# Attention's softmax blocks weighed, turned and copied four or two at a time, with smaller gate matmuls and a later conversion of query weights

## What is computed

```python
# rg_lru, 512 channels in 8 blocks of 64
r = sigmoid(block_diag_linear(x, w_a, b_a))
i = sigmoid(block_diag_linear(x, w_i, b_i))
# sparse attention: 16 heads of 64, blocks of 128 queries
proj = x @ w_in
gate = sigmoid(proj[..., 1024:])           # 16 heads x 3 branches = 48 columns
o = gate_c * o_c + gate_s * o_s + gate_w * o_w
# o_s and o_w: softmax(q k^T / 8 + relative bias, causal) v
# o_c: the same over 31 compressed keys
```

## Time and profile before

| | value |
|---|---|
| median of 3 runs | 2038.97 us (2037.82 to 2039.61) |
| the profiled execution's own time | 2038.9 us |
| its span | 2037.1 us |
| TensorE busy | 2018.7 us, 99% of the span |
| DVE busy | 1079.5 us, 53% |
| ACT busy | 829.4 us, 41% |
| GpSimd busy | 16.8 us, 1% |
| TensorE clock granted over the span | 0.996 of 2.4 GHz |

### The profile page before, as it was taken

How to read it: one execution, slowest core, us unless ns; L and a number is a source line. 1 busy time by engine, 2 the same in 40 slices (tenths; PEclk the granted TensorE clock), 3 DMA queues, 4 the chain that set the end, 5 groups by cost and what they waited for, 6 DMA issues and landing times.

```text
span 2037.1 us, 26626 instructions
## 1 busy us (share of the span) xinstructions
PE 2018.7 (99%) x10576; PEld 1697.4 (83%) x10576; DVE 1079.5 (53%) x1866; ACT 829.4 (41%) x1385; POOL 16.8 (1%) x31
## 2 busy tenths in 40 slices
PE   9999999999999999999999999999999999999998
PEld 7788888888888888889888888888788898888887
DVE  6665444443465465444744432387778666444323
ACT  5644333332334334334433322354777664333222
POOL 0000000000000000000000000000000000000000
PEclk9999999999999999999999999999999999999999
DMA  4223233323332222223233333353110023333232
GB/s 164 76 77 107 88 99 93 102 87 96 115 94 79 78 93 88 72 94 104 83 96 100 93 96 96 97 170 117 29 56 23 12 94 99 97 93 103 87 100 73
DMA packets 53546, 184.47 MB, mean 91 GB/s; under 512 B 6010, under 2 KB 8330, under 8 KB 53168
## 3 DMA queue, kind: packets, MB, share of 16 engines
q1 hardware_dynamic: 50976, 171.99, 27.4%
q0 software_dynamic: 2160, 10.63, 1.6%
q10 hardware_dynamic: 288, 0.17, 0.0%
HBM read 180.62 MB, written 2.14 MB: 90 GB/s over the span
## 4 chain that ended last, share of the span: by engine, by line
PE 93%; DVE 3%; issue 1%; ACT 1%; DVEq 0%; ACTq 0%
PE bank L518 70%; PE bank L538 6%; PE bank L687 6%; PE bank L1070 2%; PE bank L1052 1%; PE bank L927 1%; PE bank L1037 1%; PE bank L1038 1%; PE bank L915 1%; PE bank L963 1%; PE bank L1022 0%; DVE WL L1724 0%; DVE SS L2464 0%; PE bank L1023 0%; PE bank L1073 0%
## 5 line engine op out<-in xcount | busy, mean ns | idle before, releaser
L1724 DVE TENSOR_TENSOR WL<-RAW,WH 128x1024 fp32r<-128x1024 f32 (+1 forms) x320 | 384.0, 1204 | 459.1 <-ACT WH L1133 458.1
L518 PE MATMUL bank<-AH,WH 128*128 128x512 f32 x1456 | 568.5, 394 | 1.0 <-DVE XP L1779 1.0
L518 PE MATMUL bank<-AL,WH 128*128 128x512 f32 x1456 | 562.3, 390 | 0.0
L518 PE MATMUL bank<-AH,WL 128*128 128x512 f32 x1456 | 561.7, 390 | 0.0
L1133 ACT ACTIVATE WH<-RAW 128x1024 fp32r<-128x1024 f32 (+1 forms) x320 | 331.3, 1041 | 492.6 <-PE bank L518 418.4
L518 PEld LDWEIGHTS bank<-AH,WH 128*128 128x128 f32 x1456 | 273.3, 188 | 59.7 <-issue 4.0
L518 PEld LDWEIGHTS bank<-AH,WL 128*128 128x128 f32 x1456 | 273.4, 188 | 57.4
L518 PEld LDWEIGHTS bank<-AL,WH 128*128 128x128 f32 x1456 | 273.4, 188 | 55.2 <-issue 0.7
L1779 DVE TENSOR_TENSOR T<-bank,RS 128x512 f32<-128x512 f32 x156 | 106.3, 687 | 165.9 <-PE bank L518 165.9
L518 PE MATMUL bank<-HH,WH 128*128 128x512 f32 x484 | 188.3, 389 | 0.0
L518 PE MATMUL bank<-HLO,WH 128*128 128x512 f32 x484 | 188.3, 389 | 0.0
(11 more groups left out here) (400 smaller groups left out, 2835.2 us busy)
## 6 DMA issues: line engine op xcount, KB each, us to landing
RAW<-in_ffn_in SPq DMA_DIRECT2D x132, 512.0 KB, 3.6
RAW<-in_ffn_out SPq DMA_DIRECT2D x48, 512.0 KB, 3.5
RAW<-in_ret_t SPq DMA_DIRECT2D x32, 512.0 KB, 3.6
RAW<-in_ffn_out SPq DMA_DIRECT2D x24, 384.0 KB, 3.2
RAW<-in_ret_v SPq DMA_DIRECT2D x16, 512.0 KB, 3.7
RAW<-in_ret_out SPq DMA_DIRECT2D x16, 512.0 KB, 3.6
RAW<-in_w_in_t SPq DMA_DIRECT2D x13, 512.0 KB, 4.1
RAW<-in_nsa_t SPq DMA_DIRECT2D x9, 512.0 KB, 3.6
```

Of the source, the lines that this page charges most:

```text
L518: t = e.matmul(BANK[b][:, :], wt[:, sl], xx[:, slot(kk) if name == "nsa_out" else kk, :], start=kk == 0 and n == 0, stop=kk == kt - 1 and ...
L1724: e.tensor_tensor(WL[w][:, 0:n], RAW[r][:, 0:n], WH[w][:, 0:n], ALU.subtract).then_inc(w_low.did(v))
```

## The change

- **Joined blocks.** `JOINED = (4, 2, 1, 1)` by i. `lead(s)` is the first step of a joined group and `place(s)` puts the scores of a group side by side in one buffer of 512 columns. For i = 0 the four steps of a unit, for i = 1 its steps in pairs are multiplied by one DVE instruction (a tensor-by-tensor product with the weights broadcast), turned in one go of four transposes into one bank, and copied by one ACT instruction of 512 columns. For i = 2 and 3 nothing changes. DVE waits for the turn of step s - 9 only where both s and s - 9 lead a group.
- **Later query weights.** DVE's `before("nsa_t", ...)` stands two steps later (s = 4 and s % 16 = 11), the one for nsa_out at s = 107. ACT's stay.
- **Quadrant gates.** bd keeps only the 64 x 64 blocks. Each of the two matmuls of `lru_gates` becomes two of 64 rows by 64 columns. The halves of the second are swapped (rows 0 to 63 give partitions 64 to 127 and the other way round), so that the four use the four quadrants of the array. The wait for the second bank stands ahead of all four. ACT takes the second sigmoid in two instructions of 64 partitions. GpSimd clears nothing.
- **One gate tile.** For tile 8 of nsa_t DVE writes the low part of the 48 columns into columns 64 to 111 of the high part's blocks. Two passes of 8 matmuls replace three. DVE adds partitions 64 to 111 to 0 to 47 with a copy and an addition, and then scales.

The core of the diff:

```diff
@@ -367,6 +368,16 @@
         LAST = N + VALUES
+        JOINED = (4, 2, 1, 1)
+
+        def lead(s):
+
+            return s - s % JOINED[STEPS[s][1]]
+
+        def place(s):
+
+            keys = 128 * (STEPS[s][1] + 1)
+            return SS[lead(s) % NSS][:, (s - lead(s)) * keys:(s - lead(s) + 1) * keys]
...
@@ -439,13 +450,11 @@
         def pool_program(e):
-            e.memset(bd[:, :, :], 0.0).then_inc(zeroed.did("bd"))
-            e.wait_ge(*zeroed.at("bd"))
             e.wait_ge(s_x[7], 16)
...
                     rows = slice(64 * half, 64 * half + 64)
-                    e.dma_start(bd[rows, 4 * i:4 * i + 4, rows],
+                    e.dma_start(bd[rows, 4 * i:4 * i + 4, :],
                                 D[name].rearrange("(f a) i j -> a i f j", a=2)[half]).then_inc(s_bd, 16)
...
@@ -750,10 +759,12 @@
                 e.wait_ge(*lru_v.at(("conv", f)))
-                e.matmul(BANK[b][:, :], bd[:, f, :], y[:, :], start=True, stop=True).then_inc(
+                enter(b + 1, ("lru_i", f))
+                e.matmul(BANK[b][LOW, :], bd[LOW, f, :], y[LOW, :], start=True, stop=True)
+                e.matmul(BANK[b][UP, :], bd[UP, f, :], y[UP, :], start=True, stop=True).then_inc(
                     matmul.did(("lru_a", f)))
-                enter(b + 1, ("lru_i", f))
-                e.matmul(BANK[b + 1][:, :], bd[:, 4 + f, :], y[:, :], start=True, stop=True).then_inc(
+                e.matmul(BANK[b + 1][UP, :], bd[LOW, 4 + f, :], y[LOW, :], start=True, stop=True)
+                e.matmul(BANK[b + 1][LOW, :], bd[UP, 4 + f, :], y[UP, :], start=True, stop=True).then_inc(
                     matmul.did(("lru_i", f)))
...
@@ -981,9 +992,22 @@
+            def gate_tile():
+                u, b = p.first["nsa_t", 8], p.bank["nsa_t", 8]
+                w = p.slot[u]
+                enter(b, ("nsa_t", 8))
+                e.wait_ge(*w_low.at(u))
+                for kk in range(8):
+                    sl = slice(kk * 128, (kk + 1) * 128)
+                    e.wait_ge(*x_high.at(("q", kk)))
+                    e.matmul(BANK[b][:, :], WH[w][:, sl], AH[:, kk, :], start=kk == 0, stop=False)
+                    e.wait_ge(*x_low.at(("q", kk)))
+                    t = e.matmul(BANK[b][:, :], WH[w][:, sl], AL[:, kk, :], start=False, stop=kk == 7)
+                t.then_inc(matmul.did(("unit", u), ("nsa_t", 8)))
+
             for ht in range(2):
                 hidden(0, ht, range(16))
-            tile("nsa_t", 8, A, split_of("q"))
+            gate_tile()
             compressed(0)
...
@@ -1048,7 +1072,7 @@
                 e.wait_ge(*weighed.at(s))
-                for j in range(STEPS[s][1] + 1):
+                for j in range(JOINED[STEPS[s][1]] * (STEPS[s][1] + 1)):
                     t = e.transpose(b[:, ROWS[j]], SS[s % NSS][:, ROWS[j]], ident[:, :])
...
@@ -1061,20 +1085,22 @@
                     e.wait_ge(*free_a.at(("cmp", 1)))
-                e.wait_ge(*free_a.at(("turn", 4 * u + 3)))
+                e.wait_ge(*free_a.at(("turn", lead(4 * u + 3))))
                 out = [BANK[4 + f % 2][64 * hh:64 * hh + 64, ROWS[i]] for hh in range(2)]
...
                         for hh in range(2):
-                            e.matmul(out[hh], VS[:, j, c:c + 64], PT[(4 * u + 2 * br + hh) % NPT][:, ROWS[j]],
+                            v = 4 * u + 2 * br + hh
+                            e.matmul(out[hh], VS[:, j, c:c + 64],
+                                     PT[lead(v) % NPT][:, ROWS[(v - lead(v)) * (i + 1) + j]],
                                      start=br == 0 and j == 0, stop=False)
...
             for s in range(LAST):
-                if TURN <= s < N + TURN:
+                if TURN <= s < N + TURN and lead(s - TURN) == s - TURN:
                     turn(s - TURN)
...
@@ -1241,8 +1267,9 @@
                 e.wait_ge(*matmul.at(("lru_i", f)))
-                e.activation(g[:, :], BANK[b + 1][:, :], ACT.Sigmoid, bias=V("lru_bi", f)).then_inc(
-                    free_a.did(("lru_i", f)))
+                for own, other in ((LOW, UP), (UP, LOW)):
+                    e.activation(g[own, :], BANK[b + 1][other, :], ACT.Sigmoid,
+                                 bias=V("lru_bi_swapped", f)[other]).then_inc(free_a.did(("lru_i", f)))
...
@@ -1648,9 +1675,9 @@
                     compressed_values(s - 8)
-                if TURN <= s < N + TURN:
+                if TURN <= s < N + TURN and lead(s - TURN) == s - TURN:
                     v = s - TURN
-                    n = 128 * (STEPS[v][1] + 1)
+                    n = 128 * (STEPS[v][1] + 1) * JOINED[STEPS[v][1]]
                     e.wait_ge(*matmul.at(("turn", v)))
...
@@ -1721,6 +1748,11 @@
                     e.wait_ge(*w_high.at(v))
+                    if v == p.first["nsa_t", 8]:
+                        wide, raw = (t.rearrange("p (k c) -> p k c", c=128) for t in (WH[w][:, :], RAW[r][:, :]))
+                        e.tensor_tensor(wide[:, :, 64:112], raw[:, :, 0:48], wide[:, :, 0:48], ALU.subtract).then_inc(
+                            w_low.did(v))
+                        continue
                     e.tensor_tensor(WL[w][:, 0:n], RAW[r][:, 0:n], WH[w][:, 0:n], ALU.subtract).then_inc(w_low.did(v))
...
@@ -2368,8 +2400,12 @@
             e.wait_ge(*kv_a.at(("k", 7)))
-            e.tensor_tensor(T[1][0:48, :], BANK[p.bank["nsa_t", 8]][0:48, :], RS[0:48, :], ALU.mult).then_inc(
-                free_v.did(("nsa_t", 8)))
+            e.tensor_copy(T[1][0:48, :], BANK[p.bank["nsa_t", 8]][64:112, :]).then_inc(kv_v.did("low gates"))
+            e.wait_ge(*kv_v.at("low gates"))
+            e.tensor_tensor(T[1][0:48, :], T[1][0:48, :], BANK[p.bank["nsa_t", 8]][0:48, :], ALU.add).then_inc(
+                kv_v.did("gates"))
+            e.wait_ge(*kv_v.at("gates"))
+            e.tensor_tensor(T[1][0:48, :], T[1][0:48, :], RS[0:48, :], ALU.mult).then_inc(free_v.did(("nsa_t", 8)))
             e.wait_ge(*kv_a.at("kc"))
...
@@ -2459,9 +2495,9 @@
                 e.wait_ge(*matmul.at(("att", s)))
-                if s >= NSS:
+                if s >= NSS and lead(s) == s and lead(s - NSS) == s - NSS:
                     e.wait_ge(*matmul.at(("turn", s - NSS)))
-                e.tensor_tensor_reduce(SS[s % NSS][:, 0:keys], BANK[score_bank["att", s]][:, 0:keys], bias, -1.0,
+                e.tensor_tensor_reduce(place(s), BANK[score_bank["att", s]][:, 0:keys], bias, -1.0,
                                        -GUARD, ALU.add, ALU.min, NM[:, s % 8:s % 8 + 1]).then_inc(
...
@@ -2481,10 +2517,20 @@
                 _, i, hh, br = STEPS[s]
-                u, n = s // 4, 2 * hh + br
-                weighted = SS[s % NSS][:, 0:128 * (i + 1)]
+                u, n, keys = s // 4, 2 * hh + br, 128 * (i + 1)
+                weight = CF[:, u % 4, n:n + 1]
                 e.wait_ge(*weighed.at(("weights", u)))
-                e.tensor_scalar(weighted, weighted, CF[:, u % 4, n:n + 1], None, ALU.mult).then_inc(weighed.did(s))
+                if i > 1:
+                    weighted = SS[s % NSS][:, 0:keys]
+                    e.tensor_scalar(weighted, weighted, weight, None, ALU.mult).then_inc(weighed.did(s))
+                elif i == 1:
+                    weighted = SS[s % NSS][:, 0:512].rearrange("p (h k) -> p h k", h=2)
+                    by = bass.AP(weight.tensor, weight.offset, [weight.ap[0], [2, 2], [0, 256]])
+                    e.tensor_tensor(weighted, weighted, by, ALU.mult).then_inc(weighed.did(s))
+                else:
+                    weighted = SS[s % NSS][:, 0:512].rearrange("p (b h k) -> p b h k", b=2, h=2)
+                    by = bass.AP(weight.tensor, weight.offset, [weight.ap[0], [1, 2], [2, 2], [0, 128]])
+                    e.tensor_tensor(weighted, weighted, by, ALU.mult).then_inc(weighed.did(s))
...
@@ -2496,7 +2542,8 @@
                         weights_of((s - SCALE) // 4)
-                    weigh(s - SCALE)
+                    if lead(s - SCALE) == s - SCALE:
+                        weigh(s - SCALE)
                 for f in range(8):
...
@@ -2513,9 +2560,9 @@
                         query_low(query_after(s - 2 - half), half)
-                if queries_before(s):
-                    before("nsa_t", queries_before(s))
-                if s == 6 * PAIR + 9:
+                if s > 1 and queries_before(s - 2):
+                    before("nsa_t", queries_before(s - 2))
+                if s == 6 * PAIR + 11:
                     before("nsa_out", 0)
...
```

11 lines of the change are left out of this document (6 added, 5 removed).

## The result

The changed kernel takes 2042.44 us (median of 20 runs, 2037.87 to 2043.70), the kernel before 2038.18 us in the same comparison (20 runs, 2035.90 to 2040.69). The ratio is 1.0020, with a 95% interval of 1.0014 to 1.0026: the change makes the kernel 4 us slower. Forecast were 2033.2 us and a range up to 2038.0.

A forecast was written before the change was run, and what follows sets the result against it. TensorE, busy 2018.7 of 2037.1 us, was taken as the bound; 2038.9 - 2.3 (quadrant gates) - 1.8 (gate tile) - 1.6 (joined blocks and later query weights) = 2033.2 us, range 2028.0 to 2038.0.

The forecast's parts named there:

- rival A: Gate matmuls: the two row halves of a pair, writing one bank, do not overlap; 2036.5 us in all, chance 0.17.
- Part 1: Quadrant gates: a pair of gate matmuls takes 0.86 us instead of 1.72; -2.3 us, bounds -3.4 and +1.0.
- the first two places: Gate pairs after tiles 8 and 9: 0.5 us saved each, of which at most 0.89 us together arrives.
- The third place: Two gate pairs after the token-wise product: 1.72 - 0.35 = 1.4 us saved, arriving in full.
- Part 2: One gate tile: 8 of 24 matmuls go, 8 x 0.228 = -1.8 us; bounds -1.8 and 0.
- parts 3 and 4: Attention, joined blocks and later query weights: +0.9 - 0.6 - 1.5 - 0.4, about -1.6 us; bounds -8 and +8.
- 0.11 us each, alone or joined; I count nothing: Transposes in attention: their number stays 320 and each costs 0.11 us, alone or joined, so no change.
- TensorE waits 0.6 us in place of the 0.36 us that goes: Waiting for DVE's bank after the scores of step 15: +0.3 us for three of five f, -0.3 us for two.
- the first f gains the 1.15 us and perhaps half of the 0.77 us: Start of attention: TensorE's waits at 1448.93 us (1.15) and 1430.31 us (half of 0.77) go; -1.5 us in the sum.
- 0.34 us ahead of the scores of step 15: DVE's joined multiplication of step 8 takes 0.69 instead of 0.35 us, adding 0.34 us ahead of those scores.
- rival C: Attention: waits before 1450 and 1585 us shrink and TensorE keeps 2.4 GHz there; 2027.8 us, chance 0.12.
- rival B: DVE bounds steps 11 to 17, slow clock in three f: 2046.8 us, chance 0.05; milder form 2035 to 2040, 0.13.

## Why the prediction was wrong

*Right were parts 1 and 2.* The quadrants of a pair start together; rival A, the halves served one after the other, falls. Part 1 was forecast at -2.3 us; the trace shows -1.6 and so does the median of the gates alone. The mis-sized term is the first two places, 0.26 us instead of 0.9, although each is shorter by the 0.5 us of the forecast. That DVE's unit at 77 us would clip them was seen, but I took DVE's whole pause of 0.89 us as the gain. ACT's two-part sigmoids are now on the chain there, in front of DVE's work, and I had them hidden behind DVE. The third place gave 1.55 us for 1.4. Part 2 was forecast at -1.8: the trace shows -1.8, the runs -2.2.

*Wrong was the sum of parts 3 and 4*, -1.6 us forecast. The stage is 7.7 us longer; against gates and tile alone the two parts cost 8.0 us.

- The step of part 3 that failed is "0.11 us each, alone or joined; I count nothing". The price of a transpose was right and its place was left out: three of four fill waits where they stood, and ahead of step 9 they delay the scores that release DVE, 0.33 us in each of the five middle pairs, and more behind the unit of step 105. By themselves the joined blocks so cost 2.6 us in place of a gain. Beside the late unit this place costs nothing (25.5 us a pair with the turn at step 9 or 11); there the joined blocks bring 0.5 us of waits and slow stretches. The waits of the transposes for ACT that I let go did go (2.5 us to 0.2), but the values wait 2.6 us more for ACT's copies.
- The step of part 4 that failed is "TensorE waits 0.6 us in place of the 0.36 us that goes", +0.3 for three f and -0.3 for two. The wait was sized well (0.73 at the weight load, 0.49 at the matmuls) and put in the right place. But it comes in both kinds of pair, there is a second one at the next steps, and the cost is 0.36 to 0.9 us a pair, 3.5 us by the run of the late unit alone.
- The largest gain in the sum, "the first f gains the 1.15 us and perhaps half of the 0.77 us", -1.5 us, was mis-sized too. From the first scores to those of step 28 the change takes 43.37 us, before 43.78, both with two slow stretches: -0.4 us. The 1.15 us wait at 1448.93 went, but where 0.99 and 1.15 us were waited before (rows 9), two waits for DVE of 0.78 and 0.79 us and one for ACT of 0.33 stand now. The end, forecast at a gain (0.3 us in the text, 0.4 in the sum), shows none: the pair to step 124 takes 20.28 us instead of 19.73, though before has part of a slow stretch in it.
- The term "0.34 us ahead of the scores of step 15" for the joined multiplication was wrong: with single ones the pair is as long.
- The sum had no term for the clock. It stood as a gain in rival C and as a loss only in rival B. Two stretches more cost 3.2 us of the 7.7.

Rival B had the mechanism: DVE the bound in steps 11 to 17 and more slow stretches. Its strong form was too dear by 4.4 us, since the full 1.54 us a pair never came, and its mild form ended at 2040 us. The decisive number was in the profile, DVE's slack of 0.46 us against 1.2 us of work. I set it off against waits that were no cost.

## What to carry to other kernels

Where two engines answer each other through a ring of banks, ask of every instruction on which side of the releasing one it stands: ahead of it, its time is added; behind it, in the wait, it is free. Work that saves nothing by being joined should stay in that wait. A wait of a helper engine (here 1.8 us of DVE's) is no gain to be had by moving its work: the work must land in a pause, and here the pause was at step 6 and none at steps 11 to 17. Look at the waits just ahead of the smallest matmuls too: in the four kernels here that lack them, part of the time at the lower clock was gone as well.

## What the runs showed of the hardware

- Four quadrants of 64 rows by 64 columns run side by side with 512 columns each, also where two row halves write different partitions of one bank (L763 and L764 at 45.97 and 45.98 us, 0.64 us both). The Trainium skill, "TensorEngine Tiling (Array Packing)", Gotcha 1: PSUM Pressure, says that different row tiles can't access one bank simultaneously; for these writes the trace doesn't agree. Two pairs in a row take 0.43 us for each pass of four quadrants (89.92 to 90.35 us on the chain). One pass of one full-array matmul took as long, so a pair costs half.
- A stretch at 1.2 GHz lasted 3.4 us each time, twice that once (6.8 us). One in the values of step 10 cost 1.6 us. The two early ones cost 1.3 us each (43.78 us from the first scores to those of step 28 in the kernel before, 41.09 with the gates alone, whose profile has none there). In all profiles of this study they began at a few places of the stage: around steps 3 and 18, or in the small scores and the values of step 10 of a pair, once just behind them. Runs of one kernel differ by the number of them, and much of the spread of its times goes with that: in the 124 runs of before beside the experiments it took 2040.8 us on average at a clock of 0.995, 2039.4 at 0.996, 2038.5 at 0.997 and 2037.1 at 0.998.
- A wait of 0.4 to 0.5 us at a weight load is 0.18 to 0.29 us of idle matmuls, and taking it away by moving the values shortened the distance to step 11 by 0.12 us where another wait stood behind it and by 0.47 where none did.
